# The projection of p: made tile by tile in the final stage, or once in the routing block

## The reference

```python
h = h + mix @ w_out[i]
h = h + _hierarchical_moe(_rmsnorm(h, g_moe[i]), ...)
ple_gate = jax.nn.sigmoid(_rmsnorm(h, g_ple[i]) @ w_ple_gate[i])   # 1024x1024 @ 1024x1024
h = h + ple_gate * (p[i] @ w_ple_proj[i])                          # 1024x256 @ 256x1024
return _rmsnorm(h, g_final)
```

## Time and profile before

| | |
|---|---|
| runs | 1409.22, 1408.73, 1396.25 us; median 1408.73 |
| profiled execution | 1395.64 us, of it span 1393.9 us |
| TensorE busy | 1156.0 us (83%), 6357 instructions |
| VectorE busy | 623.6 us (45%) |
| ScalarE busy | 314.3 us (23%) |
| GpSimd busy | 247.8 us (18%) |
| DMA | 272.81 MB, mean 196 GB/s; 410 to 426 GB/s in most of the expert stage |
| mean granted TensorE clock | 0.915 of full speed |

### The profile page before, as it was taken

How to read it: one execution, slowest core, us unless ns; L and a number is a source line. 1 busy time by engine, 2 the same in 40 slices (tenths; PEclk the granted TensorE clock), 3 DMA queues, 4 the chain that set the end, 5 groups by cost and what they waited for, 6 DMA issues and landing times. The chain is left out here.

```text
span 1393.9 us, 17070 instructions
## 1 busy us (share of the span) xinstructions
PE 1156.0 (83%) x6357; PEld 765.5 (55%) x6358; DVE 623.6 (45%) x906; ACT 314.3 (23%) x685; POOL 247.8 (18%) x347
## 2 busy tenths in 40 slices
PE   6999999996778876998188888788897888838997
PEld 5879888875667775887133333222333333317775
DVE  5799899974656745322711111111111111154553
ACT  5211211125444534221010011000110000032232
POOL 3000100013664541000212111111211111011111
PEclk9996999998799997999589999999999988979998
DMA  6111111200000103211889999999799999961221
GB/s 200 31 46 31 46 46 46 61 0 1 1 2 1 62 2 114 91 60 61 364 315 425 425 422 423 418 410 389 310 422 423 425 424 415 378 237 60 99 98 45
DMA packets 68066, 272.81 MB, mean 196 GB/s; under 512 B 12521, under 2 KB 38314, under 8 KB 51370
## 3 DMA queue, kind: packets, MB, share of 16 engines
q1 hardware_dynamic: 56096, 254.33, 46.0%
q0 software_dynamic: 9456, 16.80, 3.2%
q10 hardware_dynamic: 2458, 0.92, 0.3%
HBM read 264.15 MB, written 25.43 MB: 208 GB/s over the span
## 5 line engine op out<-in xcount | busy, mean ns | idle before, releaser
L2216 PE MATMUL ps_u<-wup,xgT 128*64 128x512 f32 x1024 | 260.7, 668 | 59.3 <-DMA wup<-in_w_up_dram 56.8
L2216 PEld LDWEIGHTS ps_u<-wup,xgT 128*64 128x64 f32 x1024 | 86.3, 152 | 232.1 <-issue 230.9
L94 PE MATMUL ps_b<-n_hi,wh 128*128 128x512 f32 x384 | 154.3, 402 | 1.7 <-DVE wl L417 1.7
L94 PE MATMUL ps_b<-n_hi,wl 128*128 128x512 f32 x384 | 151.8, 395 | 0.0
L94 PE MATMUL ps_b<-n_lo,wh 128*128 128x512 f32 x384 | 151.7, 395 | 0.0
L2136 DVE TENSOR_TENSOR hb<-sil,ps_u 128x256 f32<-128x256 f32 x32 | 13.5, 421 | 301.7 <-ACT sil L2076 301.7
L94 PEld LDWEIGHTS ps_b<-n_hi,wh 128*128 128x128 f32 x384 | 73.1, 190 | 20.1 <-issue 2.6
L94 PEld LDWEIGHTS ps_b<-n_lo,wh 128*128 128x128 f32 x384 | 73.1, 190 | 16.6 <-issue 1.0
L94 PEld LDWEIGHTS ps_b<-n_hi,wl 128*128 128x128 f32 x384 | 73.0, 190 | 16.2
L460 DVE SCALAR_TENSOR_TENSOR convT<-upad,vecT,convT 128x1024 f32<-128x1024 f32 (+1 forms) x75 | 79.7, 1063 | 0.0
L2076 ACT ACTIVATE sil<-ps_u 128x256 f32<-128x256 f32 x32 | 12.3, 383 | 289.3 <-PE ps_u L2216 289.3
(11 more groups left out here) (365 smaller groups left out, 1973.3 us busy)
## 6 DMA issues: line engine op xcount, KB each, us to landing
wup<-in_w_up_dram SPq DMA_DIRECT2D x64, 2048.0 KB, 17.8
zT<-in_w_down_dram SPq DMA_DIRECT2D x32, 1024.0 KB, 17.3
convT<-in_w_down_dram SPq DMA_DIRECT2D x32, 1024.0 KB, 19.6
wraw<-in_w_in_dram SPq DMA_DIRECT2D x24, 512.0 KB, 4.2
convT<-y_rows SPq DMA_DIRECT2D x16, 512.0 KB, 4.6
qkvT<-in_x_dram SPq DMA_DIRECT2D x8, 512.0 KB, 8.6
qkvT<-in_w_out_dram SPq DMA_DIRECT2D x8, 512.0 KB, 5.1
xr<-in_x_dram SPq DMA_DIRECT2D x8, 512.0 KB, 3.3
```

The costliest lines, as they stand in the source:

```text
L94: ins = nc.tensor.matmul(ps, lhs[a], rhs[b], start=first and k == 0, stop=last and k == 2)
L2216: last = nc.tensor.matmul(ps_u[k][HC[c], :], xgT[k][:, j, HC[c]], wup[k][c][:, j, :], start=j == 0, stop=j == NJ - 1)
```

## The change

The product of p moves from the final stage to the routing block. There it is a plain fp32 product, with no high and low parts.

- Out projection: once `w_out` is split, SyncE loads all of p (1 MB) and `w_ple_proj` (1 MB) into the spare rows of `qkvT`.
- Routing: for each of 8 tiles TensorE makes 2 transposes and 4 fp32 matmuls (8 records) of 512 columns. ScalarE copies the transposed tile out (`p_turned`), copies the product out (`p_out`) and issues its store of 512 KB to `pp_rows` in DRAM. Tiles 0 and 1 stand ahead of the counts, tiles 2 to 4 ahead of the table product, tiles 5 to 7 behind it. From tile 2 on ScalarE waits for the store two tiles before, except in tiles 6 and 7, which have buffers of their own.
- Experts: 8 weight rows in place of 10 are loaded and split, and p isn't loaded. The first results wait for the last two stores (`s_ppl`), since they use the same rows. After `fetch_rows` SyncE waits for `s_ppl` and reads two tiles of `pp_rows` (`fetch_ple`), 512 KB each.
- Final stage: transposes, split and product of p are gone. VectorE multiplies by the row read back (`ppr`). `fetch_ple` of tile t+2 waits for the second half product of tile t. TensorE's first gate half waits for the sigmoid of the half before in place of the product with p.

```diff
@@ out projection, SyncE
+                sp.wait_ge(s_wo_lo, NJ)
+                sp.dma_start(p_all, p[0, 0].rearrange("(t q) d -> q t d", q=P)).then_inc(s_pin, 16)
+                sp.dma_start(wpp, w_ple_proj[0].rearrange("(j q) n -> q j n", q=P)).then_inc(s_pin, 16)
@@ routing, ScalarE
+                def p_turned(t):
+                    act.wait_ge(e_T, t + 1)
+                    if t >= 2:
+                        act.wait_ge(e_pp, t - 1)
+                    nc.scalar.activation(pT[t % 2][:], pq, ACT.Copy).then_inc(e_pT, 1)
+
+                def p_out(t):
+                    act.wait_ge(e_pp, t + 1)
+                    if 2 <= t < NT - 2:
+                        act.wait_ge(s_pps[t % 2], 16 * (t // 2))
+                    out_ = ppo[t] if t >= NT - 2 else ppo[t][:]
+                    nc.scalar.activation(out_, ps_pp[t % 2][:].rearrange("p h n -> p (h n)"), ACT.Copy).then_inc(e_out, 1)
+                    act.wait_ge(e_out, t + 1)
+                    act.dma_start(pp_rows[t * P:(t + 1) * P, :], out_).then_inc(s_pps[t % 2] if t < NT - 2 else s_ppl, 16)
+
                 act.wait_ge(s_rv, at["gd"])
                 nc.scalar.activation(t8["ge"][:], t8["gd"][:], ACT.Exp).then_inc(s_ra, 1)
+                p_turned(0)
+                p_turned(1)
                 act.wait_ge(s_rv, at["m2"])
                 nc.scalar.activation(t1["ex"][:], t1["m2"][:], ACT.Exp).then_inc(s_ra, 1)
+                p_out(0)
+                for t in range(2, NT):
+                    p_turned(t)
+                    p_out(t - 1)
+                p_out(NT - 1)
+                for k in G2:
+                    act.wait_ge(s_pps[k], 16 * (NT // 2 - 1))
@@ routing, TensorE
+                def p_turn(t):
+                    if t:
+                        pe.wait_ge(e_pT, t)
+                    for j in range(NJP):
+                        last = nc.tensor.transpose(pq[:, j, :], p_all[:, t, j * P:(j + 1) * P], ident[:])
+                    last.then_inc(e_T, 1)
+
+                def p_product(t):
+                    pe.wait_ge(e_pT, t + 1)
+                    if t >= 2:
+                        pe.wait_ge(e_out, t - 1)
+                    for h in G2:
+                        for j in range(NJP):
+                            last = nc.tensor.matmul(ps_pp[t % 2][:, h, :], pT[t % 2][:, j, :], wpp[:, j, HF[h]], start=j == 0, stop=j == NJP - 1)
+                    last.then_inc(e_pp, 1)
+
+                def p_products(first_, last_):
+                    for t in range(first_, last_):
+                        if t + 1 < NT:
+                            p_turn(t + 1)
+                        p_product(t)
+
+                pe.wait_ge(s_pin, 32)
+                p_turn(0)
+                p_products(0, 2)
                 pe.wait_ge(s_iota, 9)
                 pe.wait_ge(s_rv, at["ohs"])
...
+                p_products(2, 5)
                 pe.wait_ge(s_rv, at["onehots"])
...
+                p_products(5, NT)
@@ experts
-        NWJ = NJ + p.shape[3] // P
+        NWJ = NJ
...
+        def fetch_ple(sp, t, g):
+            sp.dma_start(ppr[g][:].unsqueeze(1), pp_rows[ds(t * P, P), :].unsqueeze(1)).then_inc(s_fp[g], 16)
...
+                sp.wait_ge(s_ppl, 32)
+                for g in G2:
+                    fetch_ple(sp, g, g)
...
-                    if free is not None:
-                        act.wait_ge(s_sto[k], free)
+                    act.wait_ge(s_sto[k], free) if free is not None else act.wait_ge(s_ppl, 32)
@@ final stage
-                        wait_alone(sp, f_T, t + 1)
-                        sp.dma_start(pin[g][:], p[0, 0, ds((t + 2) * P, P), :]).then_inc(s_fp[g], 16)
+                        wait_alone(sp, f_m1, t + 1)
+                        fetch_ple(sp, t + 2, g)
...
-                        dve.wait_ge(f_pp, t + 1)
+                        if h == 0:
+                            dve.wait_ge(s_fp[g], 16 + 16 * i)
                         dve.wait_ge((f_sg0, f_sg1)[h], t + 1)
-                        nc.vector.tensor_tensor(hn[g][:, HF[h]], hn[g][:, HF[h]], ps_p[:, h, :], ALU.mult).then_inc((f_m0, f_m1)[h], 1)
+                        nc.vector.tensor_tensor(hn[g][:, HF[h]], hn[g][:, HF[h]], ppr[g][:, HF[h]], ALU.mult).then_inc((f_m0, f_m1)[h], 1)
...
                     if not early(t, 1):
-                        pe.wait_ge(f_m0, t)
-                        product(ps_p, px[g], 0, NJP, 0, None)
-                        pe.wait_ge(f_m1, t)
-                        product(ps_p, px[g], 0, NJP, 1, f_pp)
-                    product(ps_g, hx[g], NJP, NJ, 0, f_g0)
+                        pe.wait_ge(f_sg0, t)
+                    product(hx[g], 0, f_g0)
                     if not last:
-                        transposes(t + 1, 1 - g, i + g)
-                    product(ps_g, hx[g], NJP, NJ, 1, f_g1)
+                        transposes(t + 1, 1 - g)
+                    if not early(t, 1):
+                        pe.wait_ge(f_sg1, t)
+                    product(hx[g], 1, f_g1)
```

More of the change, by code:

```diff
@@ L1469, in hybrid_block_kernel @@
         NRP = 96
+        PD = p.shape[3]
+        NJP = PD // P
+        pp_rows = nc.dram_tensor("pp_rows", (T, D), F32, kind="Internal").ap()
+        p_all = qkvT[:, NT + 2:NT + 4, :].rearrange("p a (t d) -> p (a t) d", d=PD)
+        wpp = qkvT[:, NT:NT + 2, :]
+        s_pin = sem("s_pin")
         with ExitStack() as c5:
@@ L1691, in hybrid_block_kernel @@
         s_iota, s_rv, s_ra, s_rp = sem("s_iota"), sem("s_rv"), sem("s_ra"), sem("s_rp")
+        e_T, e_pT, e_pp, e_out = (sem("ple_" + n) for n in ("T", "pT", "pp", "out"))
+        s_pps, s_ppl = [sem(f"s_pps{k}") for k in G2], sem("s_ppl")
         W8 = [P, NT, NG]
@@ L1715, in hybrid_block_kernel @@
             cf = sb("r_cf", [1, NOV], ctx=c6)
+            pT = [sb(f"pT{k}", [P, NJP, P], ctx=c6) for k in G2]
+            ppo = [sb(f"ppo{k}", [P, D], ctx=c6) for k in G2] * (NT // 2 - 1) + [qkvT[:, NT + 2 + k, :] for k in G2]
+            ps_pp = [psum(f"ps_pp{k}", [P, 2, 512], ctx=c6) for k in G2]
+            ps_pT = psum("ps_pT", [P, 512], ctx=c6)
             ps_pre = psum("ps_pre", [P, NT, NE], ctx=c6)
@@ L1907, in hybrid_block_kernel @@
         homes.update(pieces(N_0, NWJ))
-        sb("wg_skip", [P, 2 * D], ctx=wgs)
+        ppr = [sb(f"ppr{g}", [P, D], ctx=wgs) for g in G2]
+        sb("wg_skip", [P, 4 * D], ctx=wgs)
         homes.update(pieces(0, N_X))
@@ L2145, in result @@
                     dve.wait_ge(s_d, p + 1)
-                    if free is not None:
-                        dve.wait_ge(s_sto[k], free)
+                    dve.wait_ge(s_sto[k], free) if free is not None else dve.wait_ge(s_ppl, 32)
                     nc.vector.tensor_copy(ye[k][rows, HF[1]], ps_y[rows, 1, :]).then_inc(s_y1, 1)
@@ L2348, in high @@
                         act.wait_ge(f_g1, t - 1)
-                    if not early(t, 1):
-                        nc.scalar.activation(px[g][0][:], pq, ACT.Copy)
                     nc.scalar.activation(hx[g][0][:], ps_h[:], ACT.Copy).then_inc(f_hi, 1)
-                act.wait_ge(f_Tp, 1)
-                nc.scalar.activation(px[0][0][:], pq, ACT.Copy).then_inc(f_phi, 1)
                 square_ahead(0, 0)
@@ L2451, in _, with transposes @@
             def _(pe):
-                def turn_p(g):
-                    for j in range(NJP):
-                        last = nc.tensor.transpose(pq[:, j, :], pin[g][:, j * P:(j + 1) * P], ident[:])
-                    return last
-                def transposes(t, g, i):
-                    pe.wait_ge(s_fp[g], 16 + 16 * i)
+                def transposes(t, g):
                     pe.wait_ge(f_hn, t + 1)
@@ L2465, in transposes, with product @@
                     last.then_inc(f_T, 1)
-                def product(ps, x_, j0, n, h, done):
-                    for j in range(n):
-                        last = mm3(ps[:, h, :], [x_[0][:, j, :], x_[1][:, j, :]],
-                                   [wg[0][j0 + j][:, HF[h]], wg[1][j0 + j][:, HF[h]]], j == 0, j == n - 1)
-                    if done:
-                        last.then_inc(done, 1)
-                pe.wait_ge(s_fp[0], 16)
-                turn_p(0).then_inc(f_Tp, 1)
-                pe.wait_ge(f_plo, 1)
-                product(ps_p, px[0], 0, NJP, 0, None)
-                product(ps_p, px[0], 0, NJP, 1, f_pp)
-                transposes(0, 0, 0)
+                def product(x_, h, done):
+                    for j in range(NJ):
+                        last = mm3(ps_g[:, h, :], [x_[0][:, j, :], x_[1][:, j, :]],
+                                   [wg[0][j][:, HF[h]], wg[1][j][:, HF[h]]], j == 0, j == NJ - 1)
+                    last.then_inc(done, 1)
+                transposes(0, 0)
                 def step(t, g, i, last):
```

23 lines of the change are left out of this document (3 added, 20 removed).

## The result

Over 17 runs each, taken together, the changed kernel took **1407.37 us** (1402.41 to 1418.06) and the kernel before 1400.20 (1393.13 to 1409.63). The ratio is **1.005, 95% interval 1.0028 to 1.0071**: 4 to 10 us slower. The forecast was 1421; its range of 1400 to 1438 holds the result, but the cost is 7 us by the medians and 9.2 us in the profiled executions, a third to a half of the forecast +19. The profiled execution took 1408.37 us, span 1406.4, granted clock 0.918.

The account below looks back on a forecast made before the run. A loop round other engines was taken to bound the final stage's tiles, DMA the experts. Routing +6.0, experts -0.3, last tile -3.1, transposes -1.6, clock falls +18.0 make +19.0; on the mean 1402.4 that gives 1421 us, range 1400 to 1438.

Parts of the forecast that it names:

- What bounds the stage: Final stage: a 9.57 us loop round the other engines, not TensorE, sets the tile's time; TensorE waits about 1 us.
- the rival that TensorE is the bound: Final stage: each of 8 tiles would win 3.0 us, giving 1384 us; chance 0.07.
- Without the fall: -4.7: Final stage at full clock: 3.1 us saved in the last tile, 1.6 by dropping p's transposes in six tiles.
- The opening: Start of final stage: at most 0.5 us won by VectorE, some 0.4 lost to SyncE's two reads; zero together.
- The clock falls: +18.0: Final stage: idle of about 4 us before the transposes halves TensorE's clock, 3.0 us in each of six tiles.
- Routing: +6.0: Routing block: p's tiles and stores move the exit from 701.1 to 707; ends +2 and +15.
- The counts were to come 1.9 us late: Routing: two tiles of p ahead of the counts delay VectorE's chain from 676.10 to about 678; 6.6 if the clock stayed low.
- GpSimd's drain was to move to 703 and be covered: Routing exit: GpSimd's drain shifts to about 703, before the exit at 707, so it adds nothing.
- Carried in full by the experts: Expert stage: bound by DMA, so routing's +6 passes through in full.
- Their end was put at -0.3: Expert stage's end: two of ten weight rows fewer and no p to load, worth 0 to 0.6 us, taken as 0.3.
- The rule on queues: Routing: DMA engines alternate between SyncE's and ScalarE's queues, so stores would not stand behind weights; exit then 705.2.
- a clock that holds: Rival, final stage: no clock fall, total +1, 1403 us on the mean; chance 0.18.

Follow-up runs that it names:

- e1: Changed kernel plus 12 matmuls of no use in each of tiles 1 to 6 of the final stage, where p's product stood; 1397.16 us, ratio to before 0.9986.
- e6: Kernel before, with only the last tile's product of p made in routing, stored and read back; 1398.61 us, ratio to before 0.9992.
- e2b: Changed kernel's routing part alone: p's product made and stored but not read back, final stage as before; 1404.97 us, ratio to before 1.0043.
- e8: Changed kernel plus 6 filler matmuls a tile in tiles 1 to 6 of the final stage; 1405.88 us, ratio to before 1.0044.
- e9: e1 with two more buffers for the copied product in routing (tiles 2 and 5), reused three tiles later; 1398.35 us, ratio to before 0.9996.
- e4: Changed kernel without the eight stores of p's product and their waits, final stage reading rows of x; 1402.58 us, ratio to before 1.0014.

## Why the prediction was off, point by point

- **What bounds the stage** was right. TensorE lost 18 us of work, the tile did not get shorter by it, and TensorE's wait before the transposes grew from 1.0 to 3.9 us, which was the sign against the rival that TensorE is the bound. Where the clock held (e1, in which the filler gives TensorE its work back), the period was 15.9 us ((1369.15 - 1289.56)/5) against 16.2 before; 0.2 of the difference is the transposes of p (1.31 us from their start to the gate product, 1.09 in e1).
- **Without the fall: -4.7**; e1 shows -5.8 (141.4 against 147.2). From the start of the last transposes to the end of the span e1 takes 26.65 us (1369.15 to 1395.8), the kernel before 30.03 (1363.87 to 1393.9). That is 3.4 less, where 3.1 and 0.3 had been forecast; e6 has the same 26.7. The five periods give 1.6, forecast 1.3. The opening gives the other 0.8; it had been put at nothing.
- **The clock falls: +18.0.** This is the step that failed. All six falls came, with idle of 3.69 to 4.00 us before them, as forecast; each cost 1.7 us on average, not 3.0, together 10.4. I had the number: 8.78 against 7.09 in the earlier trace rows is 1.7, and I named it as the lower end. It was no end but the common case: of the eighteen slow up products behind a stop of more than 2.2 us in the trace of before, sixteen took 8.63 to 8.78 us (1.5 to 1.7 over), and only two took 10.04 and 10.08. I had looked at five of them. Two things made it 3.0. I took the opening of the final stage as the nearest row (8.02 against 5.49), but there the clock stayed low for six rows of 1 us, and in five of six tiles of the changed kernel for about three; only the last fall was of that kind, and it cost 2.9. And I added half a slow set of transposes (0.5) on top of a slow product. The rows of after show that the two share one low stretch: where the transposes take 1.97, the product takes 5.9 to 6.1, where they take 1.10 it takes 7.07.
- **Routing: +6.0**; measured +5.7 (e2b +5.5). The size was right, with two of its reasons wrong, so that part of the agreement is luck. The counts were to come 1.9 us late. In the profiled execution VectorE took them up 12.0 us after the block's start, as before, since the clock rose sooner than I had taken (the first product took 4.8 us, the second 3.6); in e8 and e9 the delay came, with 1.6 and 1.5 us. And GpSimd's drain was to move to 703 and be covered; it ended at 709.8, level with ScalarE, 42.4 us after the block's start; without the stores (e4) it ended after 35.8. Of the 5.7 us, e4 gives 4.4 to the stores and 1.3 to TensorE's work.
- **Carried in full by the experts**: right. They take 543.4 to 546.6 us wherever routing ends. Their end was put at -0.3, and is -1.1, which is no more than the stage differs by between executions.
- **The sum against the stages**: 19.0 - 7.6 (the falls) - 1.1 (the rest of the final stage, -5.8 in place of -4.7) - 0.8 (experts) - 0.3 (routing) = 9.2, as measured. By the medians of 17 runs it is 7.2. The median of before lay at 1400.2, and I had put the base at 1402.4.
- **The rule on queues.** The stores took 9.2 us while the weights came in, and the last down weights landed after 35.4 us in place of 27.9 (e4). The page "DMA: Bandwidth & Descriptors" of the Trainium skill (Queues, rings and completion order) lets each engine take turns between the queues: that the weights give way agrees with it. The stores do not stand behind all weights: ScalarE went on at 685.1, when the store that it had issued at 676.5 had landed, and weights issued at the block's start landed until after 700. My reading of it, an exit at 705.2 as TensorE sets it (41.1 us after the block's start), was wrong all the same: it is 42.8 us, and 38.4 without the stores. On engines that are 98% busy a store of 512 KB took 9.2 us, taking turns or not.
- **The chances**: 0.58 went to slower by over 1% and 0.35 to within 1%. With 1.7 us a fall, my own lower end, the sum is 11.2, under 14: the case within 1% was the likelier one by rows that I had. The range held the result mostly by its width: its low end had been set for a clock that holds, which it did not.

## What to carry to other kernels

Before work is taken off an engine, ask what the engine will do in the time: here TensorE's 2.75 us of product a tile was free, and it kept the clock up. If it has to go, work of no use in its place costs less than the fall (e1), and half of it isn't enough (e8). Price a clock fall by what its low stretch takes from everything in it, once, and not by instruction, and take the price from all rows of the trace that have it, not from the nearest or the worst; and where a block moves data through DMA engines that are 0.88 busy already, count the bytes first (4 MB at 400 GB/s are 10 us, here 4.4 of them on the path).

## What the runs showed of the hardware that I had not expected

- In stops of 3.7 to 4.0 us the granted clock fell near the stop's end: three times behind the start of the next transposes (0.92 in the row from 1290), three times ahead of it (0.59 in the row from 1376, TensorE starting at 1376.93). What is slow is the work behind the stop.
- Idle of 2.33 to 2.64 us before the transposes was followed by a fall in five of six cases, idle of 2.24 to 2.70 us before the up products of before by a slow product in thirteen of fourteen, and 0.97 to 1.28 us (e1) in none of six.
- The same start of the same matmuls out of a clock of 0.50 took 4.8 us in four executions (changed kernel, e1, e2b, e4) and 6.2 to 6.4 in two others (e9, e8), and the counts and the table behind it moved along by 1.5 us.
- The drain of GpSimd at a block's exit ran from 6.9 to 13.6 us with the traffic of another engine's stores (e4 against the changed kernel), the gathers that it issues being the same.
